# A hybrid decoder layer in fp32: the FFN's up products by seven half-size products a pair, its down products as a stage of their own

## What is computed

```python
def conv_ffn(hn, w_up, conv_w, conv_b, w_down):
    u = causal_dwconv(hn @ w_up.astype(hn.dtype), conv_w) + conv_b.astype(hn.dtype)
    a, b = jnp.split(u, 2, axis=-1)
    return (jax.nn.silu(a) * b) @ w_down.astype(hn.dtype)
```

## Time and profile before

| | us |
|---|---|
| median of 3 runs | 2068.86 (2068.48 to 2070.1) |
| span of the profiled execution | 2065.5 |
| PE busy in it | 2023.2 (98%) |
| DVE, ACT, POOL busy | 1183.6, 625.1, 283.3 |

### The profile page before, as it was taken

The page is one execution under the profiler, slowest core; times in us unless marked ns, Lnnn a source line. Parts: engine busy times, 40 slices in busy tenths (PEclk is TensorE's granted clock), DMA queues, the critical chain, the costliest instruction groups (busy, mean ns, idle before and its releaser), DMA issues.

```text
span 2065.5 us, 30227 instructions
## 1 busy us (share of the span) xinstructions
PE 2023.2 (98%) x12812; PEld 1940.0 (94%) x12812; DVE 1183.6 (57%) x1388; ACT 625.1 (30%) x794; POOL 283.3 (14%) x276
## 2 busy tenths in 40 slices
PE   8999999999999999999999999999999999999998
PEld 8999998999999998899999999999999999999996
DVE  6457564566667646666443342456565656565656
ACT  5223334434333444344443332211111111111113
POOL 0000003748380222122000002000000000000002
PEclk9999999999999999999999999999999999999999
DMA  9235666554555764555153211111011101110102
GB/s 281 93 104 134 144 158 204 187 189 157 164 154 133 168 182 136 167 168 157 60 186 113 92 62 52 62 62 52 31 52 52 52 31 51 52 53 31 61 31 82
DMA packets 257050, 227.10 MB, mean 110 GB/s; under 512 B 146524, under 2 KB 214468, under 8 KB 256788
## 3 DMA queue, kind: packets, MB, share of 16 engines
q1 hardware_dynamic: 256916, 225.18, 36.1%
HBM read 161.29 MB, written 63.84 MB: 109 GB/s over the span
## 4 chain that ended last, share of the span: by engine, by line
PE 88%; DVE 4%; DMA 2%; ACT 2%; issue 2%; SPq 2%; POOL 0%; POOLq 0%; DVEq 0%; ACTq 0%
PE a_psum L901 31%; PE a_psum L145 31%; PE a_psum L1172 11%; PE a_psum L888 5%; PE a_psum L976 1%; PE a_psum L994 1%; PE a_psum L1079 1%; PE a_psum L1004 1%; PE a_psum L958 1%; PE a_psum L973 1%; DMA w_raw<-in_w_in 1%; PE a_psum L1020 1%; DVE ext L1831 1%; PE a_psum L1094 1%; SPq L629 1%
## 5 line engine op out<-in xcount | busy, mean ns | idle before, releaser
L901 PE MATMUL a_psum<-xh,w_hi 128*128 128x342 f32 (+3 forms) x1656 | 535.6, 323 | 2.4 <-DVE w_lo L1523 2.3
L901 PE MATMUL a_psum<-xl,w_hi 128*128 128x342 f32 (+3 forms) x1656 | 531.4, 321 | 0.0
L901 PE MATMUL a_psum<-xh,w_lo 128*128 128x342 f32 (+3 forms) x1656 | 529.6, 320 | 0.0
L901 PEld LDWEIGHTS a_psum<-xh,w_hi 128*128 128x128 f32 x1656 | 312.2, 189 | 5.2 <-DVE w_lo L1523 3.0
L901 PEld LDWEIGHTS a_psum<-xl,w_hi 128*128 128x128 f32 x1656 | 312.4, 189 | 1.0
L901 PEld LDWEIGHTS a_psum<-xh,w_lo 128*128 128x128 f32 x1656 | 312.2, 189 | 0.0
L1226 ACT ACTIVATE w_hi<-w_raw 128x1024 fp32r<-128x1024 f32 x125 | 132.0, 1056 | 434.2 <-PE a_psum L145 409.2
L1301 ACT ACTIVATE post<-a_psum 128x342 f32<-128x342 f32 (+3 forms) x207 | 94.6, 457 | 550.0 <-PE a_psum L901 513.2
L145 PE MATMUL a_psum<-xh,w_hi 128*128 128x342 f32 (+1 forms) x1152 | 245.1, 321 | 9.2 <-DVE xl L1545 9.2
L145 PE MATMUL a_psum<-xl,w_hi 128*128 128x342 f32 (+1 forms) x1152 | 245.1, 321 | 0.0
L145 PE MATMUL a_psum<-xh,w_lo 128*128 128x342 f32 (+1 forms) x1152 | 244.2, 320 | 0.0
(11 more groups left out here) (239 smaller groups left out, 2792.4 us busy)
## 6 DMA issues: line engine op xcount, KB each, us to landing
w_raw<-in_w_in SPq DMA_DIRECT2D x76, 512.0 KB, 3.7
w_raw<-in_w_up SPq DMA_DIRECT2D x44, 512.0 KB, 3.4
mix_scratch<-post SPq DMA_DIRECT2D x32, 522.0 KB, 2.8
down_raw<-in_w_ffn_down SPq DMA_DIRECT2D x22, 512.0 KB, 4.4
ext<-mix_scratch SPq DMA_DIRECT2D x9, 1024.0 KB, 7.0
y<-mix_scratch SPq DMA_DIRECT2D x18, 512.0 KB, 5.7
ext<-grow_scratch SPq DMA_DIRECT2D x9, 512.0 KB, 4.9
ext<-mix_scratch SPq DMA_DIRECT2D x9, 512.0 KB, 6.3
```

What stands on the lines that cost most here:

```text
L901: mm = pe.matmul(psum[:, u % 2, 0:n], w[:, k, :], x[:, k, at0:at0 + n], start=(k == 0 and part == 0), stop=(k == KC - 1 and part == 2))
```

## The change

Of the 22 pairs, the first J0 = 2 stay as they were; each of the other NPAIR = 20 is done as a 2 x 2 block product by Winograd's form of Strassen's scheme. The block sizes: the pair's two tiles of 128 channels, two halves of the 1024 inputs (4 blocks k each), two halves of 516 columns (the 1026 columns are padded by XPAD = 6 on the left to 1032). Instead of eight half-size products seven are made, P0 to P6, each 4 blocks k x 3 parts x 2 pieces of 258 columns = 24 matmuls, so 168 a pair. P4 to P6 go on adding in the PSUM region that an earlier product left there. It needs these helpers:

- Once, on the activations: the norm's factor is applied to the residual in place (`x_scaled`), the unscaled residual is stored to DRAM first and comes back later; four sums of blocks (`x_sums`), and seven high and low parts of 128 x 2064 (`x_part_high` on ACT, `x_part_low` on DVE).
- Per pair, on the weights: both tiles come in one load of 1024 KB (`load_pair`), two sets of buffers; POOL makes four sums of 128 x 512 (`quarter_sum`); ACT makes seven high parts and DVE seven low parts of 128 x 512 (`quarter_high`, `quarter_split`). The low parts are written over what they were made from, so DVE's splits 0, 4 and 6 wait until POOL has all four sums.
- Per pair, on the results: ACT copies P0 out of PSUM and the finished first block (both counted by `c11`), DVE makes the other blocks in five steps of 128 x 516, each with one PSUM operand (`combine`, counted by `comb`).
- The first tap of the convolution moves from DVE to ACT (`first_tap`).

The down products no longer stand between the up products. The gated activations go to DRAM by pair (`store_act`, 512 KB), and after the last pair a stage of 2 x 22 steps q follows: a half of the tokens, an inner block kb, 8 output blocks m x 3 parts of 512 columns = 24 matmuls in eight PSUM banks. In all there are 1056 of them, as before. Each step loads 512 KB of `w_down` (so all of it twice) and 256 KB of activations, ACT makes the high parts and DVE the low parts. The last TAIL = 4 steps are taken bank by bank. The counters of some other waits are merged (`ros`, `os_`, `lev`); what waits for what stays as it was there.

The diff, cut to what matters for time:

```diff
+H2 = 516
+HP = H2 // 2
+XPAD = 2 * H2 - C_W
+J0 = 2
+NPAIR = FT - J0
+NDOWN = 2 * FT
+DW, DA, DIN = 6, 8, 3
+TAIL = 4
...
+            def load_pair(i):
+                if i == 0:
+                    sp.wait_ge(units_done, tiles_done(T_UP - 1))
+                elif i == 1:
+                    sp.wait_ge(units_done, tiles_done(T_UP + 2 * J0 - 1))
+                else:
+                    sp.wait_ge(pe_p, 7 * (i - 1))
+                sp.dma_start(u_raw[i % 2][:, :, :, :], io["w_up"][2 * (J0 + i):2 * (J0 + i) + 2].rearrange(
+                    "t p k c -> p t k c")).then_inc(pair_in(i)[0], 16)
+            def store_act(j):
+                sp.wait_ge(prod, j + 1)
+                sp.dma_start(sc["act"][j], acc_of(j, 0)).then_inc(act_st[j % 2], 16)
...
+            load_pair(1)
+            for i in range(NPAIR):
+                if 2 <= i + 1 < NPAIR:
+                    load_pair(i + 1)
+                store_act(J0 + i - 1)
+            def load_down(q):
+                half, kb = q // FT, q % FT
+                if q >= DIN:
+                    sp.wait_ge(da_hi, q - DIN + 1)
+                for early, slots, into, of in (
+                        (2, DW, dw_raw, io["w_ffn_down"][0][kb * P:kb * P + P, :]),
+                        (3, DA, da_raw, sc["act"][kb][:, 512 * half:512 * half + 512])):
+                    if slots == DA and q < FT:
+                        sp.wait_ge(act_st[kb % 2], 16 * (kb // 2 + 1))
+                    if q < slots:
+                        sp.wait_ge(pe_p, 7 * (NPAIR - 1) if q < early else 7 * NPAIR)
...
+                        sp.wait_ge(*used(q - slots))
+                    sp.dma_start(into[q % slots][:, :], of).then_inc(dn_in[q % DIN], 16)
+            load_down(0)
+            load_down(1)
+            store_act(FT - 1)
+            for q in range(2, NDOWN):
+                load_down(q)
+                if q == 5:
+                    sp.dma_start(res[:, :, 2 * H2 - SEQ:2 * H2], sc["hres"].rearrange("m p t -> p m t")).then_inc(h_in, 16)
...
-            for j in range(1, FT):
-                pe.wait_ge(w_lo, T_UP + 2 * j + 1)
-                pe.wait_ge(f_evac, 2 * j - 1)
-                if j > 2:
-                    pe.wait_ge(added, 8 * (j - 3) + 6)
-                up(j, 0, range(KC))
-                pe.wait_ge(w_lo, T_UP + 2 * j + 2)
-                pe.wait_ge(f_evac, 2 * j)
-                up(j, 1, range(KC))
-                if j > 1:
-                    pe.wait_ge(f_evac, 2 * j + 1)
-                    down_products((j - 2) // 2, j % 2)
...
+            for i in range(NPAIR):
+                for n in range(7):
+                    if i == 0:
+                        pe.wait_ge(x2_split, part_of(n))
+                    pe.wait_ge(w_lo, split_of(i, n))
+                    if i == 0 and n < 2:
+                        pe.wait_ge(f_evac, 2 * J0 - 1 + n)
+                    elif i and n == 1:
+                        pe.wait_ge(c11, 2 * i)
+                    elif i and n in (0, 2, 3):
+                        pe.wait_ge(comb, 5 * (i - 1) + (1, None, 4, 5)[n])
+                    elif n == 4:
+                        pe.wait_ge(c11, 2 * i + 1)
+                    elif n > 4:
+                        pe.wait_ge(comb, 5 * i + n - 3)
+                    hi, lo = u_high[i % 2][:, n, :, :], quarter_low(i, n)
+                    for k in range(KC // 2):
+                        for part, (w, x) in enumerate(((hi, x_high[n]), (hi, x_low[n]), (lo, x_high[n]))):
+                            for b in range(2):
+                                mm = pe.matmul(region(i, n)[:, b, :], w[:, k, :], x[:, k, HP * b:HP * b + HP],
+                                               start=(n < 4 and k == 0 and part == 0),
+                                               stop=(k == 3 and part == 2), skip_group_check=(n > 3))
+                    mm.then_inc(pe_p, 1)
+            def down_block(q, m, last):
+                half, kb = q // FT, q % FT
+                w, x = q % DW, q % DA
+                for part, (a, b) in enumerate(((dw_high[w], da_high[x]), (dw_high[w], da_low[x]), (dw_low[w], da_high[x]))):
+                    mm = pe.matmul(psum[:, m, :], a[:, m * P:m * P + P], b[:, :], start=(kb == 0 and part == 0),
+                                   stop=(kb == FT - 1 and part == 2))
+                if kb == FT - 1:
+                    mm.then_inc(d_bank, 1)
+                elif last:
+                    mm.then_inc(d_used, 1)
...
+            for q in range(NDOWN - TAIL):
+                pe.wait_ge(da_lo, q + 1)
+                pe.wait_ge(w_lo, down_of(q))
+                for m in range(KC):
+                    if q == 0 and m % 2 == 0:
+                        a = (NPAIR - 1) % 2
+                        if m // 2 == a:
+                            pe.wait_ge(c11, 2 * NPAIR)
+                        else:
+                            pe.wait_ge(comb, 5 * (NPAIR - 1) + (1, 1, 4, 5)[m // 2])
+                    if q == FT:
+                        pe.wait_ge(added, m + 1)
+                    down_block(q, m, m == KC - 1)
+            pe.wait_ge(da_lo, NDOWN)
+            pe.wait_ge(w_lo, down_of(NDOWN - 1))
+            for m in range(KC):
+                for q in range(NDOWN - TAIL, NDOWN):
+                    down_block(q, m, False)
...
+            for i in range(NPAIR):
+                j = J0 + i
+                if i:
+                    first_tap(j - 1, 1)
+                    gate_silu(j - 1)
+                act.wait_ge(pe_p, 7 * i + 1)
+                if i:
+                    act.wait_ge(comb, 5 * i - 4)
+                act.activation(pieces(u_one[:, :]), region(i, 0), ACT.Copy).then_inc(c11, 1)
+                if i == 0:
+                    x_part_high(6)
+                    gate_silu(j - 1)
+                if i + 1 < NPAIR:
+                    for n in range(4):
+                        quarter_high(i + 1, n)
+                act.wait_ge(pe_p, 7 * i + 5)
+                act.wait_ge(conv, 4 * (j - 1) + 2)
+                act.activation(pieces(u_out[0][:, 0:H2]), region(i, 0), ACT.Copy).then_inc(c11, 1)
+                if i + 1 < NPAIR:
+                    for n in range(4, 7):
+                        quarter_high(i + 1, n)
+                else:
+                    down_high(0)
+                first_tap(j, 0)
+            first_tap(FT - 1, 1)
+            gate_silu(FT - 1)
+            for q in range(1, FT + 6):
+                down_high(q)
...
+                one, two, three = (pieces(x[:, :]) for x in (u_one, u_two, u_three))
+                dve.wait_ge(pe_p, 7 * i + (2, 3, 4, 6, 7)[n])
+                if n in (1, 2, 3, 4):
+                    dve.wait_ge(comb, 5 * i + (None, 1, 2, 1, 1)[n])
+                if n > 1:
+                    dve.wait_ge(conv, 4 * (j - 1) + (None, None, 4, 2, 4)[n])
+                    dve.wait_ge(tap0, 2 * (j - 1) + (None, None, 2, 1, 2)[n])
+                if n == 0:
+                    dve.wait_ge(c11, 2 * i + 1)
+                    ins = dve.tensor_tensor(two, one, region(i, 1), ALU.add)
+                elif n == 1:
+                    ins = dve.tensor_tensor(three, two, region(i, 2), ALU.add)
+                elif n == 2:
+                    ins = dve.scalar_tensor_tensor(out=pieces(u_out[1][:, right]), in0=three, scalar=-1.0, in1=region(i, 3),
+                                                   op0=ALU.mult, op1=ALU.subtract)
+                elif n == 3:
+                    ins = dve.tensor_tensor(pieces(u_out[0][:, right]), two, region(i, 2), ALU.add)
+                else:
+                    ins = dve.scalar_tensor_tensor(out=pieces(u_out[1][:, left]), in0=two, scalar=-1.0, in1=region(i, 3),
+                                                   op0=ALU.mult, op1=ALU.subtract)
+                ins.then_inc(comb, 1)
...
+                if j == J0 - 1:
+                    x_sums(2)
+                    x_part_low(0)
+                    for n in range(4):
+                        quarter_split(0, n)
...
+            x_sums(3)
+            x_part_low(1)
+            x_part_low(2)
+            x_part_low(3)
+            for n in range(4, 7):
+                quarter_split(0, n)
+            combine(0, 0)
+            x_part_low(4)
+            combine(0, 1)
+            taps(J0 - 1, 0)
+            x_part_low(5)
+            x_part_low(6)
+            taps(J0 - 1, 1)
+            gate_product(J0 - 1)
...
+            for i in range(NPAIR):
+                j, more = J0 + i, i + 1 < NPAIR
+                if i:
+                    combine(i - 1, 4)
+                    taps(j - 1, 0)
+                    taps(j - 1, 1)
+                    combine(i, 0)
+                    gate_product(j - 1)
+                if i:
+                    combine(i, 1)
+                if more:
+                    quarter_split(i + 1, 0)
+                    quarter_split(i + 1, 1)
+                combine(i, 2)
+                if more:
+                    for n in range(2, 6):
```

(20 more changed lines are left out.)

500 lines of the change are left out of this document (316 added, 184 removed).

## The result

| | before | changed |
|---|---|---|
| median of the runs | 2069.14 us (2068.48 to 2070.1, 4 runs) | 2045.34 us (2044.92 to 2046.85, 4 runs) |
| span of the profiled run | 2065.5 us | 2043.1 us |
| mean granted clock | 0.998 | 0.991 |

The ratio is 0.9885, 95% interval 0.9871 to 0.9899: 1.15% faster. Forecast were 2039.5 us in a range of 2026 to 2060. The span fell by 22.4 us where the sum had 29.4, so 7.0 us are to be explained. The median stands 2.2 us over the span, not 3.4, which gives 1.2 of them back. In every run recorded with its span the time is some 1.8 us above it (here 2044.92 and 2043.1). By that, 1.8 of the 3.4 us of before are what lies around the span, and 1.6 say only that the profiled execution was faster than the median.

A forecast was written before the change was run, and what follows sets the result against it. PE's matmul stream was taken to bound the kernel. Span 2065.5 - 53.4 (shorter products) + 19 (entry) + 5 (down stage) = 2036.1 us, plus 3.4 from span to median: 2039.5 us, range 2026 to 2060.

The forecast's parts named there:

- PE bounds the steady pairs, and the gain is in its columns: New pairs: PE alone sets the time; shorter matmuls save 2.67 us a pair, 53.4 us over 20 pairs.
- The walk through DVE, ACT and POOL: Steady new pair: step-by-step timing of the other engines' work, claiming they cost nothing within PE's 20.0 us.
- the slack of 3.5 us at P6: Steady new pair: `combine` 2 done at 13.7 us, wanted by P6 at 17.2; the least slack.
- 119.1 ns for 258 columns: New pairs' matmuls: start-to-start distance interpolated between 118.2 ns at 256 columns and 157.5 at 342.
- Entry, 19 us: First new pair: PE waits of 16.1 us for DVE's long list plus 3 for collisions; between 12 and 30.
- collisions, +3: Entry to the new pairs: POOL's sums slow some 10 us of DVE work beside them, adding 3 us.
- Down stage, 5 us: Start of the down stage: waits of 3.3 us at step 1 and 1.5 at step 2; up to 10.
- The reload costs nothing: Down stage: the 4 MB residual reload holds back step 6 without delay, or 6 us once at half speed.
- POOL and DVE holding each other up in every pair: Rival, every new pair: POOL's sums take 12.9 instead of 5.2 us, P6 waits 4.2; 2124 us, 10%.
- Late loads: Rival, new pairs: weight loads landing after 9 us make P6 wait; at 10 us, 2060 us in all; 4%.
- Short matmuls: Rival, new pairs: 258 columns take 125 ns, so 20 us of the gain go; 2059 us, 3%.
- Seams at double cost: Rival, entry to the new pairs and down stage: together 48 us instead of 24; 2063 us, 12%.

The follow-up runs named there:

- the aligned run: Changed kernel, from the third new pair on 256 instead of 258 columns per matmul, both pieces starting on a multiple of 256 columns: 2037.74 us.
- the filling: Changed kernel plus 154 PE matmuls of 252 columns into unused PSUM columns in the pauses of the first new pair: 2041.98 us.

## Why the prediction was right, and where it was not

- **PE bounds the steady pairs, and the gain is in its columns.** Right: no PE wait in 383 us, and 2.5 us a pair between J0 = 3 and J0 = 12, near the 2.67 of the sum. The walk through DVE, ACT and POOL held within 0.3 us (a load that came 0.4 us early hid sums that took 0.3 longer), and the slack of 3.5 us at P6 was real: doubling POOL's sums broke it at that place and by the amount that the walk gives.
- **119.1 ns for 258 columns.** This step failed, the interpolation between 256 and 342 columns: measured 120.3, so 3.9 us over 19 pairs. The earlier trace rows gave the length's price, not that of the second piece's start. With 256 + 260 columns the same work takes 119.0 ns. The row of 128 columns was misread as well: its matmuls start 111 ns apart, not 106.9. No term of the sum hangs on it.
- **Entry, 19 us.** Measured 23.1. The places of the waits were right for P0, P1 and P6. The term "collisions, +3" was mis-sized: 6. It also left out the clock, 1.8 at P6. Against this my list for DVE was 0.9 us too long: without POOL's sums P6 starts at 1382.1 on the scale of before, where I had 1383.0. -0.9 + 3 + 1.8 = 3.9 of the 4.1. The small waits at P4 and P5 hardly showed (0.2 us at P5), since the products ahead of them ran slowly.
- **Down stage, 5 us.** Measured 6.0. Both waits were right: the one of 3.3 us at step 1 came at 3.4, and the one of 1.5 at step 2 was there with 1.6, hidden under the slow matmuls. What the term lacked is the clock's own 1.0.
- **The reload costs nothing.** Right: PE does not wait, though from 1790 to 1800 us the DMA share is 1.00 at 367 GB/s. The first half's sum and the adds cost 0.9 us over the bare products, where before it was 3.3; this was put down as unchanged, and it hid 2.4 us of the other errors. That the median came out only 5.8 us late is in part this luck, and in part the 1.2 us by which it moved towards the span.
- **The clock** had no term at all: 1.8 + 1.0 us of the 7.0. I priced each pause at its length, having read the windows from 1350 on, which show 1.00. The trace of before has a warning that was not read: behind a pause of 1.4 us and sixteen short matmuls its clock is 0.66 from 690 to 695, while behind one of 2.3 us at 702 it stays at 1.00.
- **The rivals.** POOL and DVE holding each other up in every pair: refuted for the steady pairs (the product takes 1.55 instead of 1.22 us, the sums up to 2.2, `combine` 2 is 3.5 us early), true at the entry alone. Late loads: they land 5.1 us after the pair's start. Short matmuls: 120.3 ns, not 125. Seams at double cost: 29 instead of 24 us with what the clock adds.

**Open**: which boundary the start of a moving operand must keep. Rows of x are 2064 bytes apart, so from one block k to the next the starts move by 16 bytes against any boundary of 32. In the aligned run the four k still take 118.2, 118.1, 118.3 and 118.0 ns: a boundary of 32 or 64 bytes is not what counts. One of 16 bytes fits all runs, if the tile itself starts on one, which is not shown. Open too: 0.4 of the 1.2 ns for 258 columns, for which the start explains 0.8. And open is what decides whether a pause of 2 to 3 us brings the clock down.

## What to carry to other kernels

Price a pause of a dense TensorE stream at up to twice its length: here 1.9 us cost 3.7 each time, and 3.4 us at the down stage cost 1.0 more than its length, since most of the slow stretch hid a later wait. Where the matmuls behind the pause are waited out anyway, the low clock costs nothing, and three pauses of about 3 us did not bring it down at all. Put the seams of a new stage where the slower engine has nothing else in its list, and keep GpSimd's tensor instructions out of a stretch in which VectorE works through SBUF operands on the critical path. When an operand is cut in two for a smaller matmul, try a cut in which both pieces start on a round address: here unequal pieces (256 + 260, the second at 1024 bytes) beat equal ones (258 + 258, the second at 1032).

## What the runs showed of the hardware

- The granted clock falls to its lower level behind a pause of TensorE of 1.94 us after a long dense stretch, 18 times of 18; the matmuls then come at half rate for about 3.7 us (doubled sums: 1531.0 to 1534.8). After a pause of 3.39 they do so for 5.4 us (1786.7 to 1792.1). But it stayed at 1.00 behind pauses of 3.06 us (with the filling, 1360.5), 2.7 (without sums, 1350) and 2.9 (J0 = 12, 1583).
- The start of the moving operand at 1032 bytes instead of 1024 costs 0.8 ns per matmul on the mean of the two pieces (118.95 against 118.15 ns at 256 columns). With pieces of 258 columns the second takes 122.0 ns, the first 118.7.
- GpSimd's sum of two blocks of 512 takes 1.29 us alone, 1.3 to 3.4 beside VectorE, whose own instructions become up to 2.2 times as long (three splits 4.08 us against 1.89). VectorE's instructions with one operand in PSUM keep their 0.69 us.
